# A hybrid conv and pooling block on eight cores: conv matrices built on GpSimd, five x tiles transposed by DMA

## The reference, cut to what matters

```python
u = rms_norm(x, mix_pre_g)
proj = u @ w_in                                    # (B, S, 5120)
a, gate, p, gates = proj[:1024], proj[1024:2048], proj[2048:3072], proj[3072:]   # columns
c = a * sigmoid(gate)                              # GLU
c = depthwise_causal_conv(c, dw_kernel, dw_bias)   # 31 taps, t-30 .. t, one filter a channel
y_conv = swish(layer_norm(c)) @ w_conv_out
z = causal_multiscale_pool(p)                      # trailing mean over 2, 4, 8, 16, minus token
z = einsum(z, pool_w) * pool_scale                 # per group of 256 channels
y_pool = z @ w_pool_out
g_conv, g_pool = split(sigmoid(gates))
h = x + rms_norm((g_conv * y_conv + g_pool * y_pool) @ w_o, mix_post_g)
v = square(relu(rms_norm(h, mlp_pre_g) @ w_ff1)) @ w_ff2
out = h + rms_norm(v, mlp_post_g)
```

## Time and profile before

| What | Value |
|---|---|
| Runs before | 973.26 us median of 3 (968.52 to 973.6) |
| Profiled execution | 973.2 us, span of core 7 971.6 us |
| Spans of the eight cores | 962.5 to 971.6 us |
| Busy: PE, DVE, ACT, POOL | 98%, 42%, 34%, 4% of the span |
| HBM read, written by the core | 127.78 MB, 16.84 MB |
| Instructions | 14273 |

### The profile page before, as it was taken

One profiled execution on the slowest core, in us unless ns is written; L12 is line 12 of the kernel. 1 busy time (PEld: TensorE's weight loads), 2 busy tenths in 40 slices (PEclk: granted clock), 3 DMA queues, 4 the chain that ended last, 5 costly groups with the idle time before them and its releaser, 6 DMA issues.

```text
span 971.6 us, 14273 instructions; the slowest of 8 cores (962.5 to 971.6 us)
## 1 busy us (share of the span) xinstructions
PE 947.4 (98%) x4990; PEld 479.7 (49%) x4990; DVE 405.3 (42%) x651; ACT 326.8 (34%) x592; POOL 42.4 (4%) x50
## 2 busy tenths in 40 slices
PE   5999999999989999999999999999999999999997
PEld 3555666775544444444444444444444444444444
DVE  3364232332647415675665541344323442333222
ACT  3565322111102492565544341133312341223211
POOL 3001000010110000010101000000000000000000
PEclk9999999999989999999999999999999999999999
DMA  9999602999999759569879994310242014210021
GB/s 193 217 218 177 77 1 46 138 155 144 126 121 177 131 123 148 112 143 234 152 195 177 201 177 109 98 65 1 66 127 93 19 26 116 96 47 1 1 87 66
DMA packets 125144, 111.69 MB, mean 115 GB/s; under 512 B 56945, under 2 KB 107377, under 8 KB 125074
## 3 DMA queue, kind: packets, MB, share of 16 engines
q0 software_dynamic: 55136, 46.45, 35.3%
q1 hardware_dynamic: 69792, 64.05, 25.7%
q10 hardware_dynamic: 146, 0.27, 0.1%
HBM read 127.78 MB, written 16.84 MB: 149 GB/s over the span
## 4 chain that ended last, share of the span: by engine, by line
PE 94%; DMA 4%; ACT 1%; issue 1%; DVE 0%; POOL 0%; DVEq 0%; ACTq 0%; POOLq 0%
PE ps L342 93%; DMA arena<-w_in 2%; DMA arena<-convw 2%; ACT arena L355 1%; PE ps L345 1%; ACT L355 0%; DVE arena L375 0%; POOL arena L378 0%; DVE arena L365 0%; DVEq L173 0%; ACT tmpA L355 0%; ACT junkb L355 0%; ACTq L140 0%; DVEq L140 0%; DVE sm L369 0%
## 5 line engine op out<-in xcount | busy, mean ns | idle before, releaser
L342 PE MATMUL ps<-arena 128*128 128x512 bf16 (+2 forms) x4560 | 916.8, 364 | 9.6 <-DMA arena<-convw 4.2
L342 PEld LDWEIGHTS ps<-arena 128*128 128x128 bf16 x4560 | 454.7, 104 | 464.3 <-issue 15.4
L355 ACT ACTIVATE tmpA<-ps 128x512 f32<-128x512 f32 x226 | 133.7, 595 | 343.2 <-PE ps L342 331.3
L358 DVE TENSOR_TENSOR arena<-tmpA 128x512 bf16<-128x512 f32 x128 | 88.2, 692 | 112.1 <-ACT tmpA L355 112.1
L358 DVE TENSOR_TENSOR arena<-ps,tmpA 128x512 bf16<-128x512 f32 x64 | 44.0, 691 | 151.8 <-ACT tmpA L355 133.5
L355 ACT ACTIVATE junkb<-ps 128x512 bf16<-128x512 f32 (+1 forms) x65 | 38.4, 591 | 177.5 <-DVE tmpA L358 112.7
L358 DVE TENSOR_TENSOR tmpA<-ps,gbt 128x512 f32<-128x512 f32 (+1 forms) x65 | 44.3, 681 | 34.3 <-PE ps L342 28.9
L355 ACT ACTIVATE junkb<-arena 128x1024 bf16<-128x1024 f32 (+1 forms) x33 | 34.6, 1050 | 60.6 <-DMA arena<-out 50.6
L358 DVE TENSOR_TENSOR sm<-sm 128x1 f32<-128x1 f32 x33 | 5.3, 160 | 108.5 <-ACT junkb L355 108.5
L355 ACT ACT_TABLE_LOAD x35 | 44.9, 1283 | 10.9 <-DVE mv L671 3.1
L355 ACT ACTIVATE arena<-ps 128x512 bf16<-128x512 f32 (+1 forms) x58 | 33.2, 586 | 36.2 <-PE ps L342 34.0
(11 more groups left out here) (40 smaller groups left out, 143.2 us busy)
## 6 DMA issues: line engine op xcount, KB each, us to landing
arena<-xh SPq DMA_DIRECT2D x32, 512.0 KB, 8.7
arena<-w_ff POOLq DMA_DIRECT2D x16, 1024.0 KB, 25.0
out<-arena SPq DMA_DIRECT2D x31, 512.0 KB, 3.0
arena<-out SPq DMA_DIRECT2D x28, 512.0 KB, 3.8
arena<-convw POOLq DMA_DIRECT2D x16, 768.0 KB, 13.0
arena<-w_in POOLq DMA_DIRECT2D x4, 1024.0 KB, 67.0
arena<-w_in POOLq DMA_DIRECT2D x2, 2048.0 KB, 22.6
arena<-w_in POOLq DMA_DIRECT2D x4, 512.0 KB, 20.3
```

The source lines that it names most:

```text
L342: kb.op("pe", lambda e: e.matmul(out_ap, lhsT=lhsT, rhs=rhs, start=start, stop=stop, skip_group_check=skip), reads=reads, writes=writes)
L355: kb.op("act", lambda e: e.activation(out=out_ap, in_=in_ap, func=func, **kw), reads=reads, writes=writes)
L358: kb.op(eng, lambda e: e.tensor_tensor(out=out_ap, in0=in0, in1=in1, op=op), reads=reads, writes=writes)
```

## The change

What the new kernel does:

- The input `convw`, the banded matrices written out (8 x 128 x 6144 floats), is replaced by `convk` (16 x 128 x 384 floats): for each window the rows of taps, without the 8x8 pattern of channels, which is zero off its diagonal. `vecs` gets eight more columns, an 8x8 identity repeated over the partitions; DVE copies it to `cmb` as bf16.
- `wk_load(w)` loads the rows (128 x 384 as bf16) into one of three buffers `kch`, which lie in `pmb`. `wc_load(w)` is now a GpSimd tensor_tensor: each tap, repeated eight times, times the identity row, 3072 elements a partition, into `Wc`; then it issues `wk_load(w + 3)`. The first three pairs stand behind GLU r = 1, since the pools before it read `pmb`.
- `Wc` has five buffers: windows 11 and 12 use two new ones in `S[1]`, and windows 13, 14, 15 use buffers 2, 0, 1. From window 8 on the matrix five places on is made. `wc_load(11)` and `(12)` are written ahead of the second half of the conv. The load of `w_conv_out` names window 15 (`("Wc", 1)`) as what it follows.
- Tiles 11 to 15 go through `a_norm_t`: the scaled row tile goes to `tmpA` and a DMA transpose of SP's queue writes `uT`. The loop at j = 7 normalizes 9 and 10, at j = 8 tiles 11 and 12, and at j = 9, 10, 11 tile j + 4.
- `w2` and `glu_load(1)` move from the head of the POOL queue to j = 11; w2 waits for tile 15's transpose.
- The silu pairs are behind groups 22, 25, 28 and 30 instead of 23, 26, 29 and 31.

```diff
-        Wc = [aview(OFF_C + 4608 + b * 3072, 3072, g=8, d=3, n=128) for b in range(3)]
+        WC_OFF = [OFF_C + 4608, OFF_C + 7680, OFF_C + 10752, OFF_S + 8192, OFF_S + 11264]
+        Wc = [aview(o, 3072, g=8, d=3, n=128) for o in WC_OFF]
...
+        for b in range(5):
+            kb.reg(("Wc", b), (WC_OFF[b], 3072))
+        kb.reg("pmb", (ARENA_N + 8192, 1216))
         for b in range(3):
-            kb.reg(("Wc", b), (OFF_C + 4608 + b * 3072, 3072))
+            kb.reg(("kch", b), (ARENA_N + 8192 + 384 * b, 384))
...
+        def a_norm_t(j):
+            n = ORDER.index(j)
+            k = next_k()
+            i = j % 4
+            src, sk = xs[:, n % 6, :], ("xs", n % 6)
+            ut = tmpA[:, i, :].bitcast(BF16)
+            ACT(junk[:, :], src, AF.Square, [sk], ["junkb", ("sm", k)], accum=sm[:, k:k + 1])
+            rs, rsk = rstd_col(128, k)
+            STT(ut, src, rs, gb[:, 0, :], ALU.mult, ALU.mult, [sk, rsk, ("gb", 0)], [("tmpA", i)])
+            DTR(uT[:, :, 128 * j:128 * j + 128], ut, [("tmpA", i)], [("ut", j)])
...
         glu_load(0)
-        wload(S[2], wpo_v, [("w2", k) for k in range(8)])
-        glu_load(1)
...
         for j in range(7, 16):
-            if j + 2 < 16:
-                a_norm(j + 2)
-            if j + 1 < 16:
+            if j == 7:
+                a_norm(9)
+                a_norm(10)
+            elif j == 8:
+                a_norm_t(11)
+                a_norm_t(12)
+            elif j + 4 < 16:
+                a_norm_t(j + 4)
+            if j + 1 < 11:
                 a_t(j + 1)
+            if j == 11:
+                wload(S[2], wpo_v, [("w2", k) for k in range(8)], after=[kb.last_write[("ut", 15)]])
+                glu_load(1)
...
+        def wc_buf(w):
+            return {11: 3, 12: 4, 13: 2, 14: 0, 15: 1}.get(w, w % 3)
+
+        kch = [pmb[:].rearrange("p g n -> p (g n)")[:, i * 384:(i + 1) * 384] for i in range(3)]
+
+        def wk_load(w):
+            wload(kch[w % 3], convk[w], [("kch", w % 3)])
+
         def wc_load(w):
-            kb.op("pool", lambda e: e.dma_start(out=Wc[w % 3].rearrange("p g d n -> p (g d n)"), in_=convw[w // 2][:, (w % 2) * 3072:(w % 2 + 1) * 3072],
-                                                max_dma_last_dim=1024), writes=[("Wc", w % 3)], dma=True)
+            b = wc_buf(w)
+            src = kch[w % 3].rearrange("p (x o) -> p x o", o=1).to_broadcast([128, 384, 8])
+            msk = cmb[:].rearrange("p (o c) -> p o c", o=1).to_broadcast([128, 384, 8])
+            TTOP("pool", Wc[b].rearrange("p g d (r c) -> p (g d r) c", c=8), src, msk, ALU.mult, [("kch", w % 3), "cmb"], [("Wc", b)])
+            if w + 3 < 16:
+                wk_load(w + 3)
...
-            if q % 2 == 1 and w + 3 < 16:
-                wc_load(w + 3)
+            nw = w + (3 if w < 8 else 5)
+            if q % 2 == 1 and nw < 16:
+                wc_load(nw)
...
-        for w in range(3):
-            wc_load(w)
+        COPY("dve", cmb[:], vec[:, 24:32], ["vec"], ["cmb"])
         for r in range(16):
             glu(0, r)
             if r in (0, 1):
                 some_pools(4)
+            if r == 1:
+                for w in range(3):
+                    wk_load(w)
+                for w in range(3):
+                    wc_load(w)
...
+        wc_load(11)
+        wc_load(12)
         interleave(groups[:12], side1, 3)
-        wload(S[1][:, :, :], wco_v, ["wco"], after=[kb.last_write[("Wc", 0)]])
+        wload(S[1][:, :, :], wco_v, ["wco"], after=[kb.last_write[("Wc", 1)]])
...
-            if n in (23, 26, 29, 31):
-                i = (n - 22) // 3
+            if n in (22, 25, 28, 30):
+                i = (n - 21) // 3
```

More of the change, by code:

```diff
@@ L164, in build_program @@
     w_ff2 = din("w_ff2", [4096, DM])
-    vecs = din("vecs", [128, 24])
+    vecs = din("vecs", [128, 32])
     gbd = din("gb", [5, DM])
@@ L168, in build_program @@
     pmd = din("pm", [128, 4 * 304])
-    convw = din("convw", [8, 128, 16 * 3 * 128])
+    convk = din("convk", [16, 128, 8 * 3 * 16])
     out = nc.dram_tensor("out", [NT, DM], F32, kind="ExternalOutput").ap()
@@ L184, in build_program @@
         epst = T("epst", [128, 2], F32)
-        vec = T("vec", [128, 24], F32)
+        vec = T("vec", [128, 32], F32)
+        cmb = T("cmb", [128, 8], BF16)
         identb = T("identb", [128, 128], BF16)
@@ L652, in cv_mm @@
             w = cc * 2 + q // 2
+            wb = wc_buf(w)
             b = nb()
@@ L656, in cv_mm @@
                 for d in range(3):
-                    MM(ps[:, b, g4 * 128:(g4 + 1) * 128], UTt[bf][:, gl, 14 + d:142 + d], Wc[w % 3][:, gl % 8, d, :], d == 0, d == 2,
-                       [("UT", bf), ("UTh", bf), ("Wc", w % 3)], [PSK(b)])
+                    MM(ps[:, b, g4 * 128:(g4 + 1) * 128], UTt[bf][:, gl, 14 + d:142 + d], Wc[wb][:, gl % 8, d, :], d == 0, d == 2,
+                       [("UT", bf), ("UTh", bf), ("Wc", wb)], [PSK(b)])
             dst = ru[:, cc, :].rearrange("p (r g c) -> p g r c", r=16, g=16)[:, q * 4:q * 4 + 4, :, :]
@@ L1016, in _pool_mats, with _conv_rows @@
     return pm.reshape(128, 4 * 304)
[L1018 to L1021, removed]
+def _conv_rows(dw_kernel):
+    k = np.asarray(dw_kernel, np.float32).reshape(31, 8, 2, 8, 8)
+    K = np.zeros((8, 2, 16, 8, 8, 3, 16), np.float32)
     for d in range(3):
@@ L1026, in _conv_mats @@
                 if 0 <= j <= 30:
-                    for c in range(8):
-                        W[:, r, c, :, d, rp, c] = kk[j, :, :, c]
-    return W.reshape(8, 128, 16 * 3 * 128)
+                    K[:, :, r, :, :, d, rp] = k[j].transpose(0, 1, 3, 2)
+    return K.reshape(16, 128, 8 * 3 * 16)
 def _prep_inputs(inp):
@@ L1034, in _prep_inputs @@
     cm = lambda v: f(v).reshape(8, 128).T
-    vecs = np.zeros((128, 24), np.float32)
+    vecs = np.zeros((128, 32), np.float32)
+    vecs[:, 24:32] = np.tile(np.eye(8, dtype=np.float32), (16, 1))
     vecs[:, 0:8] = cm(inp["conv_ln_g"])
@@ L1044, in _prep_inputs @@
     shared["ident"] = np.eye(128, dtype=np.float32)
-    shared["convw"] = _conv_mats(inp["dw_kernel"])
+    shared["convk"] = _conv_rows(inp["dw_kernel"])
     maps = []
```

## The result

The changed kernel takes 975.88 us (median of 20 runs, the kernel before 971.85 in 20): 1.0038 of the time of before, 95% interval 1.0027 to 1.0048. It is slower by 0.4%, where 0.9% faster was forecast; 975.9 lies above the range. (A few executions of either kernel, up to 1161 us, were disturbed; the ratio leaves them out.)

What follows compares the result with a forecast made beforehand. PE, busy 98% of the span, was taken as the bound, with the slowest core setting the time. Core 7's terms, -6.9 - 2.25 - 0.96 + 0.5 = -9.6 us, gave 963.6, core 4 965.2; forecast 964.5 us, range 960.5 to 973.

Steps and rivals of the forecast that it cites:

- What bounds the kernel: Whole kernel: PE busy 98% of the span, slowest core sets the time; only removing PE work or gaps pays.
- part 1: Conv matrices: 16 loads of 768 KB become 16 of 96 KB, no late landing; 6.9 us gained on core 7.
- Core 7's 6.9 us: PE gap at 278.7 us behind a conv matrix load: 4.15 us plus 2.8 us of lower clock behind it.
- Part 2, the period: GpSimd expansion of conv matrices: 6.2 us multiply, 0.6 issue of the row load, 0.1 wait; 6.9 us a matrix.
- The limit of 7.8 us: Conv matrices on GpSimd: longest time per matrix that still keeps PE supplied, set by nine matrices in 70.4 us.
- Rival A: Conv matrices: GpSimd sets the pace and PE waits; 969 to 972 us at 8.3 a matrix, 991 at 10; chance 0.20.
- Cost on the path: nothing: GpSimd expansion of conv matrices: every matrix ready before PE wants it, 8 us of slack at matrix 15; 0 us.
- rival C: Conv halo copies: DVE and GpSimd block each other; one multiply's wait costs nothing, two 1.5 us each, 976.5; chance 0.04.
- The 10.9 us of PSUM banks: Conv halo copies: PE can run 10.9 us while DVE waits, three of eight banks being filled in 4.13 us.
- Parts 3 to 5: x tiles 11 to 15 by DMA: 2.25 us gained, 0.5 lost; later w2 and GLU loads: 0; earlier silu: 0.96 gained.
- The sum: Core 7: -6.9 - 2.25 - 0.96 + 0.5 = -9.6 us, time 963.6; core 4 965.2; forecast between them 964.5 us.
- the sums of two cores: Whole kernel: 963.6 us for core 7 and 965.2 for core 4; the forecast lies between them.

Runs made afterwards that it cites:

- the conv part, cured: Kernel before with only the conv change, halo copies on ScalarE and first GpSimd multiplies behind fold_scale: 966.32 us, ratio 0.9947 to the kernel before.
- the lock cured: Changed kernel with halo copies moved from DVE to ScalarE and first three GpSimd multiplies behind fold_scale: 964.06 us, ratio 0.9915 to the kernel before.

## Why the prediction was wrong, step by step

- **What bounds the kernel, and part 1.** Right in kind, too large in size. Core 7's 6.9 us were one execution's; over more runs the conv part, cured, is worth 0.9947, some 5.2 us.
- **Part 2, the period.** 6.9 us forecast, 6.47 measured: the multiply took 5.31 us and not 6.2, the wait on its own engine 0.54 and not 0.1. The limit of 7.8 us lies, as it should, between the 6.47 us that left PE without a wait for GpSimd and the 8.72 us that made it wait; no run is nearer to it. Rival A did not come. The estimate from the Trainium skill's GPSIMD Engine Reference (Performance versus the Vector engine), 6.7 us, was too high for these bf16 views: 5.31 us is 1.73 ns an element.
- **The step that failed** is "Cost on the path: nothing" in part 2, together with rival C's price and its chance of 0.04. C named the mechanism and the halo copies. It then reckoned with one multiply (nothing lost) or two (1.5 us at each place), which makes 976.5 over eight places. That this is near the measured 975.9 is luck: one copy cost a gap of 5.4 us on every core and up to 2.8 of clock behind it, the other seven cost nothing, and the rest came from fold_scale. Three things were missed. The row load behind a multiply is its pause, and the last three have none, which can be read in the diff; so a copy issued in the first of three stood for what was left of that one and for two more, 11.5 us. The 10.9 us of PSUM banks (11.0 by its own figures) take a stage with fewer conv pieces, and count from the moment at which PE begins a bank with all others free: here eight banks lasted 9.6 us, and 2.1 of them were gone when the copy was issued, so PE stopped 7.5 us after it (257.57 to 265.05). And fold_scale, moved by nothing, now shares its stretch with the first three multiplies; it was not priced at all, and is worth 4.3 us of the time.
- The Trainium skill's SBUF — State Buffer (Who interferes with whom) has the kind of wait right: the pair of ports is held for a whole instruction, and a DVE instruction with two SBUF inputs contends with a GpSimd one that reads SBUF. The trace agrees in that the maximum of two SBUF inputs stood as long (11.55 us) as the copy (11.54), and that the products from PSUM run beside a multiply at 0.69 us. The length is more than that rule gives, 11.5 us for a multiply of 5.3. Nor did the one that was issued first always get the pair, as the page has it: a scaling issued at 127.73, 0.43 us ahead of a multiply, stood until that multiply ended.
- **Parts 3 to 5.** Right: DMA transposes of the tiles landed in 3.4 us (median), w2 in 18.8, no PE gap at tiles 11 to 15 but 0.45 us more for ScalarE's eviction at 76 us, and the silu gap gone. They are worth about 3.1 us once the conv part is cured, where 2.7 were forecast.
- **The sum.** Forecast 8.7 us below the profiled run; with the lock cured 0.9915, 8.3 us of 972.3. The sum is met within 0.4 us, in part by luck: its largest term was 1.7 too much (5.2 us where 6.9 had been put on core 7), the rest gave some 0.4 more than was put, and the forecast took the middle between the sums of two cores. The one mechanism held at nothing cost 12 us (975.68 against 964.06).

## What to carry to other kernels

Before arithmetic goes to GpSimd, list the DVE instructions in the same stretch that are copies, tensor_scalars or two-input operations within SBUF, and ask for each what stands behind it on DVE. The wait may be not one GpSimd instruction but the whole run of them without a pause, so let a DMA issue or a semaphore wait fall between, or move the few DVE ones to ScalarE. A pause only cuts the run: several DVE instructions in a row, such as fold_scale's, meet the next GpSimd instruction all the same, and if PE is close behind them the GpSimd work has to go elsewhere in time. A resource counted from its full size (eight banks) must be counted from where it stands at that moment.

## What was not expected of the hardware

A GpSimd instruction that is already queued takes over from the one before at once, past a waiting DVE instruction: the copy had waited 0.9 us when the second multiply began and 6.2 us when the third did, and the three ran in 15.83 us, 5.28 each, as if nobody waited. With about 1.1 us between them the copy got in at the first pause.

A pause is not open in all its length. In the changed kernel, the scalings issued 0.89 us ahead of the next multiply ran in 0.35 to 0.36 us, and so did one issued 0.53 us ahead (121.15 on core 5, 0.34 us), beside the issue of a row load; such an issue does not by itself keep DVE out. But on all eight cores one was issued 0.42 to 0.43 us ahead of a multiply, also during such an issue, and stood 5.9 us. Why it lost is open.
